# First head of a windowed-attention layer: a projection cut by feature tiles and laid between the pieces of the attention

## The reference, cut to what matters

```python
def odd_layer(x, norm_w, w_in, w_out, sink, cos, sin):
    h = rmsnorm(x, norm_w)
    proj = jnp.einsum('bsd,de->bse', h, w_in)
    qc, kc, vc, gc = split_cols(proj, ODD_SIZES)
    oc = window_gqa_with_sink(qc, kc, vc, sink, cos, sin) * jax.nn.silu(gc)
    return jnp.einsum('bse,ed->bsd', oc, w_out)
...
    # in window_gqa_with_sink, for one block of 128 queries:
    s = jnp.where(valid, s, -jnp.inf)
    m = jnp.maximum(jnp.max(s, axis=-1, keepdims=True), sink_g)
    p = jnp.exp(s - m)
    p = p / (jnp.sum(p, axis=-1, keepdims=True) + jnp.exp(sink_g - m))
    return jnp.einsum('bhgqk,bkhd->bqhgd', p.astype(vx.dtype), vx)
```

## Time and profile before

| | |
|---|---|
| Time of the kernel, median of 3 runs | 1210.87 us (1208.26 to 1211.58) |
| The profiled execution's own time | 1211.01 us |
| Its span, first to last instruction | 1209.1 us |
| PE busy | 1148.0 us, 95% of the span |
| DVE busy | 952.1 us, 79% |
| ACT busy | 666.5 us, 55% |
| Mean granted clock of TensorE | 0.982 of full |
| The odd layer's first head on PE | from about 777 to 824 us of the span |

### The profile page before, as it was taken

How to read it: one execution, slowest core, us unless ns; L and a number is a source line. 1 busy time by engine, 2 the same in 40 slices (tenths; PEclk the granted TensorE clock), 3 DMA queues, 4 the chain that set the end, 5 groups by cost and what they waited for, 6 DMA issues and landing times. The chain is left out here.

```text
span 1209.1 us, 18540 instructions
## 1 busy us (share of the span) xinstructions
PE 1148.0 (95%) x5750; PEld 923.7 (76%) x5750; DVE 952.1 (79%) x1882; ACT 666.5 (55%) x1299; POOL 0.2 (0%) x4
## 2 busy tenths in 40 slices
PE   4989999999999999999999977988999999999996
PEld 3767778778778778787887755877888888888876
DVE  6678778878878878887797877567887887878886
ACT  5365555564555554654554634356566655656663
POOL 0000000000000000000000000000000000000000
PEclk7999999999999999999999998998999999999998
DMA  6521512522324215215215103533332323322111
GB/s 195 145 82 53 140 53 62 147 68 64 111 69 115 76 52 139 69 43 130 69 52 140 36 1 93 121 93 79 108 87 52 87 53 107 100 73 87 53 36 70
DMA packets 131672, 103.07 MB, mean 85 GB/s; under 512 B 5424, under 2 KB 116400, under 8 KB 131632
## 3 DMA queue, kind: packets, MB, share of 16 engines
q1 hardware_dynamic: 131632, 102.54, 31.0%
HBM read 77.36 MB, written 2.10 MB: 66 GB/s over the span
## 5 line engine op out<-in xcount | busy, mean ns | idle before, releaser
L74 PE MATMUL bank_proj<-hH,w_hi 128*128 128x512 f32 x576 | 230.4, 400 | 3.8 <-DVE hL L140 3.8
L76 PE MATMUL bank_proj<-hH,w_lo 128*128 128x512 f32 x576 | 225.7, 392 | 0.0
L75 PE MATMUL bank_proj<-hL,w_hi 128*128 128x512 f32 x576 | 225.2, 391 | 0.0
L74 PEld LDWEIGHTS bank_proj<-hH,w_hi 128*128 128x128 f32 x576 | 108.8, 189 | 26.4 <-issue 5.3
L76 PEld LDWEIGHTS bank_proj<-hH,w_lo 128*128 128x128 f32 x576 | 108.6, 189 | 23.7
L75 PEld LDWEIGHTS bank_proj<-hL,w_hi 128*128 128x128 f32 x576 | 108.9, 189 | 21.3
L74 PE MATMUL bank_odd_proj<-hH,w_hi 128*128 128x512 f32 x288 | 117.2, 407 | 5.1 <-DVE hL L140 4.4
L75 PE MATMUL bank_odd_proj<-hL,w_hi 128*128 128x512 f32 x288 | 113.5, 394 | 0.0
L76 PE MATMUL bank_odd_proj<-hH,w_lo 128*128 128x512 f32 x288 | 113.5, 394 | 0.0
L1027 DVE TENSOR_TENSOR w_lo<-w_raw,w_hi 128x1024 fp32r<-128x1024 f32 x73 | 88.8, 1217 | 17.1 <-ACT w_hi L597 17.1
L597 ACT ACTIVATE w_hi<-w_raw 128x1024 fp32r<-128x1024 f32 x75 | 78.9, 1054 | 36.4 <-DMA w_raw<-in_w_in_even 33.3
(11 more groups left out here) (352 smaller groups left out, 2440.2 us busy)
## 6 DMA issues: line engine op xcount, KB each, us to landing
w_raw<-in_w_in_even SPq DMA_DIRECT2D x72, 512.0 KB, 4.7
w_raw<-in_w_in_odd SPq DMA_DIRECT2D x36, 512.0 KB, 4.7
qs<-parts SPq DMA_DIRECT2D x96, 128.0 KB, 2.3
ks<-parts SPq DMA_DIRECT2D x40, 256.0 KB, 4.2
o_raw<-in_w_out_even SPq DMA_DIRECT2D x16, 512.0 KB, 4.9
o_raw<-in_w_out_odd SPq DMA_DIRECT2D x14, 512.0 KB, 6.7
out<-w_raw SPq DMA_DIRECT2D x8, 256.0 KB, 2.1
mixT<-in_x SPq DMA_DIRECT2D x2, 512.0 KB, 5.8
```

Of the source, the lines that this page charges most:

```text
L74: pe.matmul(out, hi, moving_hi, start=start, stop=False)
L75: pe.matmul(out, hi, moving_lo, start=False, stop=False)
L76: return pe.matmul(out, lo, moving_hi, start=False, stop=stop)
```

## The change

`proj` takes a range of feature tiles, `first` to `end`, in place of a half. Where `outs` is true the calls give the same halves as before. Where it is false, which is in the two halves of the first head only, projection `n + 1` is cut into five pieces: tiles 0 and 1 before `values(0)`, tile 2 behind it, tile 3 after `scores(2)`, tile 4 after `values(1)`, tiles 5 and 6 after `scores(3)`, tile 7 after `values(2)`. No other engine's list is touched, and the number of instructions is the same.

```diff
--- before.py
+++ after.py
@@ -1340,20 +1340,19 @@
 
         @block.tensor
         def _(pe):
-            def proj(h, n, half=None):
+            def proj(h, n, first=0, end=KT):
 
                 bank, use = bank_of(n)
-                if half != 1:
+                if first == 0:
                     if w_low.due(h, n):
                         pe.wait_ge(w_low.sem, w_low.at(h, n))
                     if bank.free.due(h, use - 1):
                         pe.wait_ge(bank.free.sem, bank.free.at(h, use - 1))
                 s = (n + 5) % SLOTS
-                tiles = range(KT) if half is None else range(half * KT // 2, (half + 1) * KT // 2)
-                for k in tiles:
+                for k in range(first, end):
                     mm = split_product(pe, bank[:], w_hi[s][:, k], w_lo[s][:, k], hH[:, k], hL[:, k],
                                        k == 0, k == KT - 1)
-                if half != 0:
+                if end == KT:
                     mm.then_inc(bank.full.sem, 1)
 
             def scores(h, half, t):
@@ -1448,34 +1447,45 @@
                 if not first:
                     turns(h_before, before, 3)
                 if first:
-                    proj(h, n, 0)
+                    proj(h, n, 0, 4)
                 scores(h, half, 0)
                 if not first:
-                    proj(h, n, 0)
+                    proj(h, n, 0, 4)
                 if not first:
                     values(h_before, before, 3, group if half else group_before)
-                proj(h, n, 1)
+                proj(h, n, 4, 8)
                 turns(h, half, 0)
                 scores(h, half, 1)
                 if not first:
                     turn_weight(h_before, before, turn_of(half, outs))
-                proj(h, n + 1, 0)
+                proj(h, n + 1, 0, 4 if outs else 2)
                 values(h, half, 0, group)
-                proj(h, n + 1, 1)
+                if outs:
+                    proj(h, n + 1, 4, 8)
+                else:
+                    proj(h, n + 1, 2, 3)
                 turns(h, half, 1)
                 scores(h, half, 2)
                 if outs:
                     out_tile(h, 4 * half, 5 * half + 2)
+                else:
+                    proj(h, n + 1, 3, 4)
                 values(h, half, 1, group)
                 if outs:
                     out_tile(h, 4 * half + 1, 5 * half + 3)
+                else:
+                    proj(h, n + 1, 4, 5)
                 turns(h, half, 2)
                 scores(h, half, 3)
                 if outs:
                     out_tile(h, 4 * half + 2, 5 * half + 4)
+                else:
+                    proj(h, n + 1, 5, 7)
                 values(h, half, 2, group)
                 if outs:
                     out_tile(h, 4 * half + 3, 5 * half + 5)
+                else:
+                    proj(h, n + 1, 7, 8)
 
             def iteration(h, group, group_before, zeroth=False, last=False):
```

## The result

| | before | after |
|---|---|---|
| Median | 1210.99 us (1208.26 to 1211.58, 4 runs) | 1202.81 us (1201.04 to 1203.78, 4 runs) |
| Ratio, 95% interval | | 0.9935 [0.9916, 0.9954] |
| Span of the profiled execution | 1209.1 us | 1199.0 us |
| Mean granted clock | 0.982 | 0.987 |

What follows compares the result with a forecast made beforehand. PE, busy 95% of the span, was taken as the bound, with winnable waits and low clock around the first head. Terms of -2.73 and -2.69 us sum to -5.42, from 1211.01 to a forecast of 1205.5 us, range 1203.5 to 1208.7.

Steps and rivals of the forecast that it cites:

- DVE's wait: First head, DVE idle before `low_turn(1)`: an earlier `turns(1)` wins 1.88 us in the first half, 0.99 in the second.
- `rotate` what was late next: DVE in the first head: `rotate` does not move, so `low_turn(1)` follows its end, at 787.6 in the first half.
- Tile 7: Between `values(2)` and `turns(3)` in both halves: adds 0.70 us each, net +0.12 and +0.08 with full clock there.
- The half behind the head: Second head's first half: at full clock it goes from 27.80 to 26.02 us, a gain of 1.78.
- The softmax, the queries' DMA and `silu`: First head's surroundings: softmax of tile 1 just in time at 784.95, queries land before they are asked for, `silu` delays nobody.
- The size in the head: First head and the half after it: -2.73 us by the first half, -2.69 by the second, -5.42 together.
- the range: Whole kernel: 1203.5 to 1208.7 us, from the forecast less run spread up to both cases of partial gain.
- The step ahead of it: Whole kernel: 5.42 taken from the profiled 1211.01 us, 0.14 above the median, gives 1205.6; from the median 1205.45.
- The first rival: Clock falls in the second half's longer wait: 6.8 us low costs 2.3, gain 3.1, 1207.7 us; chance 0.26.
- a low clock between 789 and 828: First head and the half after it: full clock expected; low clock again in this stretch would show the forecast wrong.
- The Trainium skill's rule: PE clock: going through PSUM banks with small waits makes the clock swing, so the low clock would return.
- The slower case: Clock falls before `values(1)` in both halves and stays low: 3.1 us slower, 1214.1 us; chance 0.05.

## Why the prediction was wrong

- **The mechanism was right but for the clock of the second half.** DVE's wait was what could be won, -1.88 and -0.99, and `rotate` what was late next: `low_turn(1)` follows it without a bracket, and splitting `rotate` frees 3.3 us more. Tile 7 costs its 0.70 twice. The half behind the head is 26.07 us where 26.02 was written. The softmax, the queries' DMA and `silu` made nobody wait.
- **The size in the head was right**: 5.42 forecast, 5.34 in the first pair. Part of that is luck: the profile that it was worked out from had one of the two long heads. Over all profiles it is 73.49 (mean of four) less 68.63 (mean of three), 4.9 us.
- **The failed step is the range**: "The range goes from 1203.5 (the forecast less what runs of one kernel differ by: the lowest is 2.6 below the median)". It took the spread of three runs for that of the kernel, and then reached only 2.0 below; 2.6 below is 1202.9, and 1202.81 would have missed that too. It put at nothing, without a reason, what the stretches outside the head differ by from one execution to the next. 35 runs of before went from 1205.21 to 1216.23 us, 25 of the changed kernel from 1200.51 to 1210.45. The step ahead of it has the same fault: it set the sum against one profiled execution as if 0.14 us from a median of three made it typical. In thirteen profiles of kernels whose instructions are the same up to `scores(0)` that stretch took from 774.05 to 780.27 us (782.31 in a fourteenth), and the last one either 43.5 to 43.6 or 45.0 to 45.2. The first pair fell apart on both: 3.2 and 1.6 us.
- **Against the larger samples the forecast is near, and they are wide.** All 36 runs of the three copies of before have a mean of 1210.4 us, all 25 of the changed kernel 1204.8: 5.6 us. In medians it is 1210.3 and 1203.8, just inside the range. The forecast was 1205.5. But these runs come from several groups, and within each the means differ by 7.8, 7.2 and 3.0 us. Three ratios, 0.9935, 0.9941 and 0.9972, are compatible with one effect of 0.9954 (the quotient of the two means) seen through that scatter; it is the upper end of the first interval. The whole kernel's time alone does not fix the gain closer than that; the head does.
- **The first rival's condition came true and its price did not.** The prediction took full clock for the likelier case and named a low clock between 789 and 828 as a sign that it is wrong. That sign came: the clock fell behind the second half's longer wait, in all three profiles of the changed kernel. In the first:

```profile
810.19:813.61 3.42, 3.42 (x16) 2.80 (x14) 1.27 (x3) 2.84 (x8) 0.00 (x0) 0.50 0.85 209
```

That is 3.4 us, not the 6.8 that I priced it at. Nor did it cost half its length. With the second half alone cut, where the clock was high there, `values(1)` to `values(2)` took 6.01 us with 1.05 of waiting; here it took 6.29 with 0.29. So PE's work grew by 1.0 us, not 1.7, the wait took 0.8 of it, and 0.3 is left (0.2 to 0.3 in the three profiles), in place of 2.3.

That the wait of 2 us makes the clock fall is not shown either. With the second half alone cut the same wait (1.97), and with tile 7 early one of 2.00, had no fall behind it, in one profile each. What decides is open. The Trainium skill's rule ("TensorE: Matmul & The Clock Gate", "A second HAM failure mode: psum-queue depth-cycling"), which the prediction weighed as the ground for this rival, is not borne out by the pattern itself: the first half of the changed kernel goes through the banks in the same way at 1.00, and so do both halves where `rotate` is split.

- **The slower case** had no trace in any run.
- **What stays open**: why the stretch ahead of the odd layer differs by up to 8 us between executions. The low clock is part of it at most. From 700 to 777 us the granted clock was 0.93, 0.91, 0.89 and 0.87 in executions where the stretch took 774.34, 777.50, 780.27 and 782.31 us. But it was 0.96 in the two with 774.05 and 778.35 us, and 0.93 in nine, which took from 774.26 to 776.82. I did not try to change it.

## What to carry to other kernels

When one engine's list puts a whole block ahead of the step that the others wait for, cut the block and lay its pieces in that engine's own waits; what is won is the others' idle time up to whatever is next in their lists, not the time of the pieces moved, and here also what the higher clock gave. Then look at that next thing (here `rotate`), and at pieces that still lie outside a wait (here tile 7): they were worth almost as much as the change. And judge a change of half a per cent by the stretch that holds it, cut at events that both profiles have; the span of one pair of profiles, or four runs, can be off by as much as the effect.

## What was not expected of the hardware

- The same code takes different time in steps, not smoothly: the last head 43.5 or 45.1 us, the first head of before 73.0 or 74.0, with the granted clock as the column that differs (0.95 and 0.93 in the first head, where one low stretch is 3.4 or 6.8 us long).
- A fall of the clock to half can be nearly free: 3.4 us of it ahead of a wait of 1 us cost 0.2 to 0.3 us. And the same wait of 2 us had a fall behind it in three profiles and none in two.
- Thirty redundant matmuls made the head 1.6 to 2.6 us shorter in the one profile of them; the clock was 1.00 through it. In the whole kernel's time the runs don't show it (ratio 0.9990 [0.9970, 1.0010]).
